# Moving a GpSimd addition behind the last low part, and two splits ahead of a gate pair, in a fused decoder layer

## The reference

```
x = x + RMSNorm_post(concat(y_A, y_B) @ W_o)          # W_o: 1024 x 1024
h = RMSNorm_pre_ffn(x)
ff = silu(h @ w_gate) * (h @ w_up)                     # 1024 x 2816 each
x = x + RMSNorm_post_ffn(ff @ w_down)                  # 2816 x 1024
```

## Time and profile before

| | |
|---|---|
| time, median of 3 runs | 679.45 us (679.12 to 680.95) |
| the profiled execution's own time | 680.61 us |
| its span, first to last instruction | 678.9 us |
| PE busy | 664.6 us (98%) |
| DVE busy | 480.9 us (71%) |
| ACT busy | 318.4 us (47%) |
| POOL busy | 95.4 us (14%) |
| mean granted TensorE clock | 0.995 of full |

### The profile page before, as it was taken

How to read it: one execution, slowest core, us unless ns; L and a number is a source line. 1 busy time by engine, 2 the same in 40 slices (tenths; PEclk the granted TensorE clock), 3 DMA queues, 4 the chain that set the end, 5 groups by cost and what they waited for, 6 DMA issues and landing times.

```text
span 678.9 us, 10102 instructions
## 1 busy us (share of the span) xinstructions
PE 664.6 (98%) x4077; PEld 593.0 (87%) x4077; DVE 480.9 (71%) x657; ACT 318.4 (47%) x511; POOL 95.4 (14%) x130
## 2 busy tenths in 40 slices
PE   8999999999999999999899999999999989999996
PEld 6878888888988889888898999999999988888885
DVE  6766999998978677348876888889888653423325
ACT  6656334443268676236343645546555352231312
POOL 4800310000316385002300000000000000000000
PEclk9999999999999999999899999999999999999999
DMA  8453032432522303150222232333343233322303
GB/s 271 126 165 115 5 120 80 136 127 66 184 62 67 120 2 125 63 185 1 75 71 97 70 126 77 110 125 90 97 125 100 88 112 109 121 90 96 124 1 124
DMA packets 49375, 68.69 MB, mean 101 GB/s; under 512 B 5041, under 2 KB 39857, under 8 KB 49330
## 3 DMA queue, kind: packets, MB, share of 16 engines
q1 hardware_dynamic: 45760, 60.16, 27.8%
q0 software_dynamic: 3280, 7.35, 3.1%
q10 hardware_dynamic: 290, 0.55, 0.2%
HBM read 65.40 MB, written 4.74 MB: 103 GB/s over the span
## 4 chain that ended last, share of the span: by engine, by line
PE 92%; DVE 4%; ACT 2%; issue 1%; DMA 1%; POOL 0%; DVEq 0%; POOLq 0%; ACTq 0%
PE PS L1445 53%; PE PS L1785 26%; PE PS L1664 2%; PE PS L1519 2%; PE PS L1495 1%; PE PS L1494 1%; PE PS L1675 1%; DVE A L1277 1%; ACT A L832 1%; PE PS L1598 1%; PE PS L1489 1%; DVE A L1271 1%; DMA A<-in_x_dram 1%; DVE A L1268 1%; PE PS L1560 1%
## 5 line engine op out<-in xcount | busy, mean ns | idle before, releaser
L1445 PE MATMUL PS<-hT_lo,w_hi 128*128 128x512 f32 (+2 forms) x280 | 102.6, 366 | 0.0
L1445 PE MATMUL PS<-hT_hi,w_lo 128*128 128x512 f32 (+2 forms) x280 | 101.2, 361 | 0.0
L1445 PE MATMUL PS<-hT_hi,w_hi 128*128 128x512 f32 (+2 forms) x280 | 101.1, 361 | 0.0
L1377 DVE TENSOR_TENSOR W_r<-W_f,s_w 128x2048 fp32r<-128x2048 f32 x11 | 25.2, 2292 | 64.0 <-ACT s_w L889 64.0
L1445 PE MATMUL PS<-s_w,ff_lo 128*128 128x512 f32 x176 | 68.5, 389 | 0.0
L977 DVE TENSOR_TENSOR w_lo<-raw,w_hi 128x2048 fp32r<-128x2048 f32 x21 | 48.1, 2291 | 19.5 <-ACT w_hi L653 19.4
L1785 PE MATMUL PS<-hT_hi,W_r 128*128 128x256 f32 x216 | 61.1, 283 | 0.0
L1785 PE MATMUL PS<-hT_hi,s_w 128*128 128x256 f32 x216 | 61.1, 283 | 0.0
L1785 PE MATMUL PS<-hT_lo,s_w 128*128 128x256 f32 x216 | 61.1, 283 | 0.0
L1445 PEld LDWEIGHTS PS<-hT_hi,w_hi 128*128 128x128 f32 (+1 forms) x280 | 53.1, 189 | 8.5
L1445 PEld LDWEIGHTS PS<-hT_lo,w_hi 128*128 128x128 f32 (+1 forms) x280 | 53.2, 190 | 7.4 <-issue 0.2
(11 more groups left out here) (250 smaller groups left out, 1649.9 us busy)
## 6 DMA issues: line engine op xcount, KB each, us to landing
raw<-in_w_in_dram SPq DMA_DIRECT2D x15, 1024.0 KB, 5.5
W_f<-in_w_down_dram SPq DMA_DIRECT2D x11, 1024.0 KB, 4.9
W_f<-in_w_gate_dram SPq DMA_DIRECT2D x9, 1024.0 KB, 5.3
W_f<-in_w_up_dram SPq DMA_DIRECT2D x9, 1024.0 KB, 5.2
raw<-in_w_o_dram SPq DMA_DIRECT2D x4, 1024.0 KB, 5.0
A<-in_x_dram SPq DMA_DIRECT2D x4, 512.0 KB, 5.4
A<-in_x_dram POOLq DMA_DIRECT2D x4, 512.0 KB, 5.7
raw<-in_w_gate_dram SPq DMA_DIRECT2D x2, 1024.0 KB, 5.3
```

What stands on the lines that cost most here:

```text
L1377: dve.tensor_tensor(lo, view(ring3(NS + d), J_DN + d), hi.bitcast(F32), ALU.subtract).then_inc(s_dlo, 1)
L1445: o = pe.matmul(out, lhs[a], rhs[b], start=(first and n == 0), stop=(last and n == 2))
```

## The change

Three places. On POOL, the addition that makes xsum waits for all four low parts of x2 instead of for the first two. On ACT, in the last of the 18 rounds, the high part of the first ff pair is taken before the high part of the first down weights and before the last pair of sigmoids, instead of behind them. On DVE, in the same round, the low part of the ff pair and then that of the down weights come ahead of `take(16)`, instead of behind it (down first). No instruction is added or removed.

```
# POOL
-            pool.wait_ge(s_hlo, TB + 2)
+            pool.wait_ge(s_hlo, 2 * TB)
             pool.tensor_tensor(xsum, hT_hi[:, :, 0:S // 2]..., hT_lo[:, :, 0:S // 2]..., ALU.add).then_inc(s_xs, 1)
# ACT, round n
                 pass_on(n, 0)
                 if n + 1 < NS:
                     sums_to_hi(n + 1)
                 else:
+                    ff_hi(0)
                     down_hi(0)
                 if n % 2:
...
                 pass_on(n, 1)
                 if n + 1 < NS:
...
                     last_hi(n + 1)
-                else:
-                    ff_hi(0)
# DVE, round n
                 if n + 1 < NS:
                     columns_lo(n + 1, 0)
                     sums_lo(n + 1)
+                else:
+                    ff_lo_pair(0)
+                    down_lo(0)
                 if n:
                     take(n - 1)
                 if n + 1 < NS:
                     columns_lo(n + 1, 1)
-                else:
-                    down_lo(0)
-                    ff_lo_pair(0)
```

## The result

| | before | changed |
|---|---|---|
| median of the runs | 680.20 us (4 runs, 679.12 to 681.18) | 674.75 us (4 runs, 674.63 to 675.58) |
| profiled execution, own time and span | 680.61, 678.9 | 674.63, 672.8 |
| PE busy | 664.6 | 663.4 |
| mean granted clock | 0.995 | 0.998 |

The ratio is 0.9923, with a 95% interval of 0.9903 to 0.9943: faster by 3.9 to 6.6 us.

A forecast was written before the change was run, and what follows sets the result against it. The prediction took PE's idle time and lower clock as the bound: 2.91 (wait) + 1.59 (clock) = 4.50, plus 1.80 from the last round, 6.30 in all; 679.45 - 6.30 = 673.15 us, predicted as 673.2, range 672.0 to 675.8.

The forecast's parts named there:

- What bounds the kernel: Whole kernel: PE is busy 664.6 of 678.9 us, so time falls only where PE stands still or runs slower.
- The long norming of block 3: DVE's line 1277 takes 5.60 us because POOL's addition runs beside it; moving the addition brings it to 1.28.
- Gain of 2.91 in the wait: PE's block 3 transposes start at 327.47 instead of 330.38 once POOL's addition is moved: 2.91 us.
- Gain of 1.59 in the clock: Block 3's transposes and following matmuls: without idle time no lower clock, 3.75 us instead of 5.34.
- Slack of the row sums, 0.3: Before chunk J_FF + 2: sums ready at 342.4, PE arrives at 342.74, so the moved addition costs nothing, barely.
- rival 2: Late row sums or a late take(16) make a new wait: gain only 5 to 5.8 us, 673.7 to 674.5; chance 14%.
- Second edit, 1.80: Last round: PE's first w_down matmul starts at 548.58 instead of 550.38, gaining 1.80 us, 0.18 of stall left.
- "No clock comes back" at the second gap: Before w_down: removing the gap gains nothing from the clock, since the granted clock behind it was 1.00.
- The sum: Whole kernel: 4.50 + 1.80 = 6.30 us gained; profiled execution 674.3, median 673.15.
- The DMA (1): Line 1277 is slowed by a landing weight chunk, not POOL; only 1.80 us gained, 677.7; chance 4%.
- The late row sums (3): Before chunk J_FF + 2: sums so late that the kernel gets slower, 680.9 if the addition takes 11 us; chance 2%.
- Rival 4: One place fails, the clock falls anyway or the ff pair isn't ready: gain 4.4 to 4.7, 674.8 to 675.0; chance 5%.

The follow-up runs named there:

- e1: Kernel before with only POOL's addition moved behind the last low part, last round in its old order: ratio to before 0.9940, median 676.95 us.
- e4: Kernel before with POOL's addition replaced at its old place by a memset that only writes: ratio to before 0.9949, median 677.82 us.
- e7: Changed kernel with POOL's addition waiting only for block 3's norming, so it runs beside the low parts: ratio to before 0.9908, median 674.54 us.
- e5: Kernel before with 28 idle transposes filling PE's wait for block 3: ratio to before 0.9986, median 679.94 us.
- e2: Changed kernel with POOL's addition back at its old place, so only the last round's order is changed: ratio to before 0.9962, median 678.99 us.
- e6: Changed kernel with POOL's addition also waiting for DVE's split of chunk J_FF + 2: ratio to before 0.9919, median 675.34 us.
- e8: e7 with ACT's last sigmoids before the down weights' high part, and DVE's take(16) before their low part: ratio to before 0.9904, median 674.12 us.
- e3: Changed kernel with ACT's half of the last-round edit undone, DVE keeping the new order: ratio to before 0.9990, median 679.95 us.
- e10: Kernel before with only POOL's addition moved behind the last low part, timed a second time: ratio to before 0.9947.
- e12: Kernel before, unchanged, profiled a third time: span 681.0 us, mean granted clock 0.993.

## Why the prediction was right

**What bounds the kernel.** Right: with the two waits gone the span is shorter by what they and the clock behind the first had cost, and C to end moved by only 0.07.

**The long norming of block 3.** Right, shown by e1, e4 and e7. It costs 1.28 without POOL's reads beside it.

**Gain of 2.91 in the wait.** Right: the fourth group of transposes starts 3.75 behind the third in the changed kernel, 6.66 before.

**Gain of 1.59 in the clock.** The mechanism is right (e5: 1.44 back with the wait kept). The size was read from one execution and taken for all. Measured over executions it is 1.4 to 2.8 where the fall comes, and by the times it seems to be 0 in at least 16 of 54 runs of before and in 5 of 12 of e2.

**Slack of the row sums, 0.3.** The distance is right, 342.97 - 342.70 = 0.27, and PE didn't wait. But not all of it was slack: the prediction left out the 0.15 that PE needs after the last sum, and e6 shows 0.12 of real slack. So it came closer to rival 2 than the text says. Each date of the chain was off by less than 0.1, with 0.24 for the later start taken out: the addition at 330.91 (said 330.9), the split at 331.40 (331.40), its end at 337.67 (337.6), the sums at 342.46 (342.4). POOL's order before DVE decided it, as said; the full wait by the Trainium skill's page (SBUF — State Buffer, "Who interferes with whom") and the row of before gave almost the same end, and the trace lies between, 2.14 behind POOL against 2.10 and 2.29. The Trainium skill's warning on GpSimd spans (Perfetto Trace Analysis, "GPSIMD Engine Instruction") didn't bite here: the addition shows 4.57 and 4.62 in two places, and DVE's rows agree.

**Second edit, 1.80.** Measured 203.14 - 201.38 = 1.76. The last thing that PE needs is take(16), the third in the row, as said (it ends at 544.20, PE starts at 544.35, and e8, which puts it second, closes the gap); 0.21 of the gap stays (said 0.18). That ACT's half costs nothing is right, and e3 shows that without it PE starts w_down 3.5 later.

**"No clock comes back" at the second gap.** Wrong as a rule: right in the first profile only. The gap brings 1.55 in some executions (e5, e10, e12), and the edit takes these away as well.

**The sum.** 680.61 - 6.30 = 674.31 was to be the profiled execution's time, and it was 674.63; 0.24 of the 0.32 is the later start. The distances give 4.51 + 1.76 + 0.07 = 6.34. The median was to fall to 673.15 and is 674.75, within the range. The step that was off is the last one: I took the median to lie 1.16 below the profiled execution after the change as it had before. Of the three runs shown two belong to the lowest group, without the fall or most of it, and the changed kernel has no such spread to draw on: 679.4, the median of the lowest group of before, less 2.91 and 1.76 is 674.7; three of its four runs lie at 674.63 to 674.85, the fourth at 675.58. Its median is 4.7 below that group, 5.6 to 6.9 below the middle one and 7.2 to 8.3 below the highest. That the range held is in part its width: it had been drawn for the spread of the runs, and the miss of 1.55 in the median would have left a narrow one.

**The rivals.** The DMA (1) fell with e4 and with the split held up at a DMA share of 0.00. A new wait (2) did not come; the gap left at w_down was 0.03 longer than said. The late row sums (3) did not come: POOL kept 4.62 with the split behind it. Rival 4 foretold 674.8 to 675.0 and so lies nearer to the median than my forecast, but the trace excludes it: the clock stays at 1.00 and the ff pair is ready in the gap. The median alone would have misled.

## What to carry to other kernels

Look at what starts together with a long instruction, not only at what it waits for: a side engine's addition that nobody needed for 12 us cost PE 2.9 us and in many executions a lower clock by starting 0.06 ahead of the one DVE instruction that PE was waiting for. Move it to where the same collision meets work with slack, or, as e7 does, beside instructions that don't collide with it. And price idle time of PE from several executions: what the clock adds differs from one execution to the next, so a gap removed narrows the spread of the times as well as lowering them (679.1 to 683.1 in 54 runs of before, 673.9 to 675.6 in the 13 runs of the changed kernel, e7 and e8).

## What was not expected of the hardware

With one and the same program, idle time of PE brought the lower level of the clock, 1.2 GHz, in some executions and not in others. Behind the 2.1 us gap before w_down it came in three of seven profiled executions (e5, e10 and one of the three of before; not in e1 and e4) and cost about 1.55 each time; behind the 2.9 us wait it came in all four profiles in which that wait stood empty and cost 23.29 - 21.92 = 1.4 to 24.68 - 21.92 = 2.8 (21.92 is 19.01 and the 2.91 of waiting); by the times it stayed away in five of e2's twelve runs. In e6 a wait of 0.6 brought none.
